# First-block attention of a two-block transformer kernel: heads zero-padded to 128 partitions, cumulated gates as extra contraction rows

## The chip, the cores and the metric

The kernel runs on one core of a Trainium2 chip. The metric is device time in microseconds of one launch. The kernel before has a median of 1077.13 us over three runs (1076.63 to 1077.66).

## The reference

The program computes two transformer blocks over 256 tokens of width 1024, in f32. Only the first block's mixer matters here. From the normalised input it makes, among others, queries, keys and values of eight "fox" heads of width 64 and queries of eight sliding-window ("swa") heads that share two key/value heads. The fox heads carry a forget gate: the logarithms of its sigmoid are summed over the sequence, and the difference of these sums is added to the scores.

```python
log_f = jax.nn.log_sigmoid(f_logit + f_bias)        # [256, 8 heads]
c = jnp.cumsum(log_f, axis=1)
logits = jnp.einsum('bqhd,bkhd->bhqk', qi, k) * HEAD_DIM ** -0.5
logits = logits + ci.transpose(0, 2, 1)[..., None] - c_k[:, :, None, :]
logits = jnp.where(causal, logits, NEG_INF)
p = jax.nn.softmax(logits, axis=-1)
out = jnp.einsum('bhqk,bkhd->bqhd', p, v)
```

The swa heads add a table bias and a sink to the softmax instead. Both outputs, with a short convolution, then go through gated output products.

## The kernel before

**Weights.** All matrices stream from memory in units of up to 1 MB (2048 columns of 128 partitions). SyncE loads a unit into one of three `raw` buffers as soon as VectorE has finished with the unit three before it (`fetch`). ScalarE rounds it to fp32r (`hi`, the line L1192), VectorE forms the rest (`lo`, L1785, a `tensor_tensor` of two SBUF inputs), and TensorE multiplies three times: high by high, high by low, low by high. In the program text both helpers convert unit u+2 where TensorE works on unit u. L547 is a feature-major unit (4 tiles of 128 columns, moving 256 tokens), L606 a token-major one (moving 512 columns).

**Order.** Every engine has its own hand-written sequence. TensorE goes: the fq units, fk, fv, svf (swa keys and values and the forget logits, 272 columns), sq, then cc, cu, cb (the convolution's inputs) and six gates of two units each.

**The gates' sums.** ScalarE copies svf's result out of PSUM (L1296, L1297). TensorE turns keys and logits over (L848, L849), VectorE adds the bias (L1887), ScalarE takes abs, exp and ln (L1301 to L1305), and a scan on VectorE gives `cumc`, [16 x 256] with the eight heads twice (L1893). Inside the second sq unit, TensorE turns `cumc` over (`cumulated_turned`, L838) into per-token columns `ct`.

**The head loop.** Sixteen heads, eight fox and then eight swa, are pipelined through slots: `attention(t)` stands on each engine behind the unit of slot t. On TensorE it holds `values(t-4)` (L819, L821), `probs(t-3)`, three transposes of the probabilities (L806), `scores(t-1)` (L787, L788) and, for fox heads, `decay(t)`. A fox head's queries and keys are 64 partitions of a tile that holds two heads, so the scores contract over 64 rows; the values have 64 columns and write 64 PSUM partitions. `decay` (L797) multiplies a [16 x 128] selection `oneh` (one row of -1, written by eight instructions at L1878) with `cumc`, which spreads the negated sums over 128 partitions. VectorE adds `ct` and the causal mask to it (`decays`, L1906, L1908) into `MC`, which `softmax` on VectorE (L1925, L1926) then adds to the scores while it takes the row maxima. ScalarE takes exponentials (L1315, L1316), VectorE scales (L1940, L1941), ScalarE copies the turned probabilities (L1323), and after every second head ScalarE and VectorE split the output of the pair (L1331, L1807). `values` of an even head waits for that split of the pair before; `scores` and `decay` wait for the maxima two heads before. Between its slots VectorE also does the whole convolution (L1977 to L1998), and ScalarE the gates' tanh (L1359).

**Evacuations.** `evac` on VectorE (L1825, L1827) multiplies four tiles of PSUM, [128 x 1024], by the row norms into fq, fk and sq. `evac_tm` on ScalarE (L1237) copies fv in two instructions of 512 columns. GpSimd has no program of its own.

## Time and profile before

| | us |
|---|---|
| median of three runs | 1077.13 |
| span of the profiled execution | 1075.8 |
| TensorE busy | 1065.3 (99%) |
| its weight port busy | 956.6 (89%) |
| VectorE busy | 752.9 (70%) |
| ScalarE busy | 602.0 (56%) |
| GpSimd busy | 0.2 |
| mean transfer rate | 170 GB/s |

PE is TensorE's multiply row, PEld its weight loads, DVE VectorE, ACT ScalarE, POOL GpSimd, SPq SyncE's queue of transfers. An f32 product appears as two records (two passes), so "L787 x2" is one product. In a shape such as 64*128 64x256 the first pair is contraction rows times stationary columns and the second the moving tile. "idle before <- releaser" in brackets tells what an engine last waited for. The mixer's head loop lies between 66 and 215 us of the span; the rest of the kernel is not touched by the diff.

### The profile page before, as it was taken

To read this page: it belongs to the slowest core of one execution; us is meant where nothing else is said; L and a number is where in the kernel's file an instruction comes from. 1 tells how busy PE (TensorE), PEld (TensorE's weight loads), DVE (VectorE), ACT (ScalarE), POOL (GpSimd) and SP (SyncE) were. 2 spreads that over 40 slices of the span, in tenths; PEclk is the share of its full clock that TensorE was granted. 3 is DMA by queue.
4 is the path that set the end of the run, shared out by engine and by line. 5 is a ranking of instruction groups with operands and counts; after the bars stand their busy time and mean duration, and the time that the engine had idled before them with its cause. 6 is when DMAs were issued, how large, how long until landed. Compare 5 with 4: busy or idle time off the path is not lost.

```text
span 1075.8 us, 16238 instructions
## 1 busy us (share of the span) xinstructions
PE 1065.3 (99%) x6866; PEld 956.6 (89%) x6866; DVE 752.9 (70%) x906; ACT 602.0 (56%) x731; POOL 0.2 (0%) x4
## 2 busy tenths in 40 slices
PE   8999999999999999999999999999999999999998
PEld 8988777789998988888889989999999888888887
DVE  5566855476745478777568898679947888776556
ACT  5454365543535465555446986589555665555444
POOL 0000000000000000000000000000000000000000
PEclk9999999999999999999999999999999999999999
DMA  9774244565553456664655545443544646654551
GB/s 303 187 223 153 79 157 157 161 191 194 171 183 118 156 178 224 195 191 153 212 189 176 154 143 167 143 151 125 157 158 148 196 141 212 196 193 160 198 174 40
DMA packets 141448, 183.08 MB, mean 170 GB/s; under 512 B 14132, under 2 KB 91936, under 8 KB 141376
## 3 DMA queue, kind: packets, MB, share of 16 engines
q1 hardware_dynamic: 141160, 181.85, 53.3%
q8 instruction: 54, 0.88, 0.3%
q10 hardware_dynamic: 216, 0.21, 0.1%
q14 instruction: 18, 0.15, 0.0%
HBM read 180.79 MB, written 1.25 MB: 169 GB/s over the span
## 4 chain that ended last, share of the span: by engine, by line
PE 93%; DVE 3%; ACT 2%; DMA 1%; issue 1%; DVEq 0%; ACTq 0%
PE ps L547 29%; PE ps L575 22%; PE ps L606 15%; PE ps L577 11%; PE ps L1012 3%; PE ps L652 2%; PE ps L1139 2%; PE ps L654 1%; PE ps L819 1%; DVE wlo L1785 1%; DMA raw<-in_w_in 1%; PE ps L806 1%; PE ps L788 1%; PE ps L901 1%; PE ps L1027 1%
## 5 line engine op out<-in xcount | busy, mean ns | idle before, releaser
L1785 DVE TENSOR_TENSOR wlo<-raw,whi 128x2048 fp32r<-128x2048 f32 (+3 forms) x170 | 378.3, 2228 | 163.6 <-ACT whi L1192 163.2
L1192 ACT ACTIVATE whi<-raw 128x2048 fp32r<-128x2048 f32 (+1 forms) x167 | 310.4, 1862 | 86.3 <-PE ps L577 34.2
L547 PE MATMUL ps<-ha,whi 128*128 128x256 f32 x1328 | 244.7, 286 | 2.3 <-DVE wlo L1785 2.2
L575 PE MATMUL ps<-ha,whi 128*128 128x512 f32 x640 | 222.7, 394 | 0.0
L547 PEld LDWEIGHTS ps<-ha,whi 128*128 128x128 f32 x1328 | 208.2, 193 | 6.5 <-issue 5.2
L547 PE MATMUL ps<-ha,wlo 128*128 128x256 f32 x664 | 188.5, 284 | 0.0
L577 PE MATMUL ps<-ha,wlo 128*128 128x256 f32 x640 | 177.4, 277 | 0.0
L575 PEld LDWEIGHTS ps<-ha,whi 128*128 128x128 f32 x640 | 120.0, 188 | 27.9
L547 PEld LDWEIGHTS ps<-ha,wlo 128*128 128x128 f32 x664 | 128.0, 193 | 0.0
L575 PE MATMUL ps<-pr,whi 128*128 128x512 f32 x352 | 122.1, 394 | 0.0
L577 PEld LDWEIGHTS ps<-ha,wlo 128*128 128x128 f32 x640 | 120.2, 188 | 0.1
L606 PE MATMUL ps<-whi,ha 128*128 128x512 f32 x320 | 100.6, 395 | 0.0
L577 PE MATMUL ps<-pr,wlo 128*128 128x256 f32 x352 | 97.5, 277 | 0.0
L575 PEld LDWEIGHTS ps<-pr,whi 128*128 128x128 f32 x352 | 66.0, 188 | 15.3
L606 PEld LDWEIGHTS ps<-whi,ha 128*128 128x128 f32 x320 | 58.7, 188 | 14.7 <-issue 3.3
L577 PEld LDWEIGHTS ps<-pr,wlo 128*128 128x128 f32 x352 | 66.1, 188 | 0.0
L606 PE MATMUL ps<-wlo,ha 128*128 128x512 f32 x160 | 62.5, 390 | 0.0
L1463 ACT ACTIVATE silu<-silu 128x512 f32<-128x512 f32 x22 | 13.9, 633 | 62.1 <-DVE silu L2124 62.1
L1458 ACT ACTIVATE silu<-ps 128x512 f32<-128x512 f32 x22 | 13.1, 598 | 41.8 <-PE ps L577 35.7
L606 PEld LDWEIGHTS ps<-wlo,ha 128*128 128x128 f32 x160 | 30.0, 188 | 6.6
L1012 PE MATMUL ps<-qt,kt 128*128 128x128 f32 x256 | 31.2, 275 | 0.4 <-DVE am L2242 0.4
L1012 PEld LDWEIGHTS ps<-qt,kt 128*128 128x128 f32 x256 | 30.3, 192 | 0.9 <-issue 0.6
(385 smaller groups left out, 1687.4 us busy)
## 6 DMA issues: line engine op xcount, KB each, us to landing
raw<-in_w_in SPq DMA_DIRECT2D x54, 1024.0 KB, 5.3
raw<-in_w_ffn_gate SPq DMA_DIRECT2D x11, 1024.0 KB, 5.1
raw<-in_w_ffn_up SPq DMA_DIRECT2D x11, 1024.0 KB, 5.2
raw<-in_w_gate SPq DMA_DIRECT2D x11, 1024.0 KB, 5.2
raw<-in_w_up SPq DMA_DIRECT2D x11, 1024.0 KB, 5.2
raw<-in_w_xkv SPq DMA_DIRECT2D x8, 1024.0 KB, 5.2
raw<-in_w_ffn_down SPq DMA_DIRECT2D x8, 1024.0 KB, 5.0
raw<-in_w_down SPq DMA_DIRECT2D x8, 1024.0 KB, 5.0
```

Of the source, the lines that this page charges most:

```text
L547: mm = e.matmul(ps[0:width, m * T:(m + 1) * T], a[:, kk, m * width:(m + 1) * width], b[:, off + k, :], start=k == 0 and j == 0 and m % 2 = ...
L575: e.matmul(banks[s][:, at_:at_ + 512], wh[:, kk, c], H[2][:, :, k, :], start=k == 0, stop=False, skip_group_check=True)
L577: mm = e.matmul(banks[s][:, at_ + T:at_ + 512], wl[:, kk, c], H[0][:, k, :], start=False, stop=k == K - 1, skip_group_check=True)
L606: mm = e.matmul(banks[s][:, t * 512:t * 512 + ncol], b[:, off + k, t * P:(t + 1) * P], a[:, kk, 0:ncol], start=k == 0 and j == 0, stop=k = ...
L652: e.matmul(banks[ss[i]][:, at_:at_ + 512], wh[:, k, c], H[2][:, :, k, :], start=k == 0, stop=False, skip_group_check=True)
L654: mm = e.matmul(banks[ss[i]][:, at_ + T:at_ + 512], wl[:, k, c], H[0][:, k, :], start=False, stop=k == 7, skip_group_check=True)
L1012: mm = e.matmul(Sb[w][:, m * P:(m + 1) * P], Kt[b][:, m, w * P:(w + 1) * P], Q_[:, m, wq_ * P:(wq_ + 1) * P], start=m == 0, stop=True, ski ...
L1139: mm = e.matmul(where, x[:, k, t_ * P:(t_ + 1) * P], w[:, kk, a:b], start=k == 0 and j == 0, stop=k == 7 and j == 2, skip_group_check=True)
L1192: e.activation(h, r, ACT.Copy).then_inc(*hi_done.up(n))
L1458: e.activation(silu[w][:, :, :], split_sums(ss[2 * (i % 2)])[1], ACT.Copy).then_inc(*a_evac.up(f"{b}g{i}"))
L1463: e.activation(silu[w][:, :, :], silu[w][:, :, :], ACT.Silu).then_inc(*a_stat.up((f"silu {b}", i)))
L1785: e.tensor_tensor(l, r, h.bitcast(F32), ALU.subtract).then_inc(*lo_done.up(n))
```

## The change

Each fox head gets a query tile, a key tile and a value tile of 128 partitions or columns: even heads use the lower half, odd heads the upper, and the other half is padding, so queries and keys become two tiles each (`fq[u]`, `fk[u]`, u the parity), as do fv, sq and sv. Four rows of the other half of each fox query and key tile carry the sums: in the key tile four rows hold the negated `cumc` of the four heads of that parity, against which the query tile has rows that are one for its own head and zero elsewhere; and the other way round for the query's own sums. The scores therefore come out of one product with the sums already in them. `decay`, `decays`, `cumulated_turned`, `oneh`, `ct` and `MC` go; `softmax` adds the plain causal mask `M3`.

A new program on GpSimd writes the pads: one-and-zero rows from the identity (four `tensor_copy` of [64 x 1024]) and zeros (six `memset` of a tile half, and one of `skf`). VectorE evacuates fq, fk and sq in two halves of 64 partitions (`evac_heads`) and writes the key sums; ScalarE writes fv in four instructions, svf in ten, and the query sums. The logits, their turning and the sums are now [128 x 256] tiles of which 16 rows count. The forget bias is loaded by four small transfers behind a wait for a memset of its column. The scores, 16 swa and fox alike, contract over 128 rows; all values have 128 columns, and the second head of a pair accumulates onto the first in the same PSUM tile. The first scores now wait for the key sums, the query sums and the pads.

```diff
+    OWN = [slice(0, 64), slice(64, 128)]
+    OTHER = [slice(64, 128), slice(0, 64)]
+    KEY_ROWS = [slice(64, 68), slice(0, 4)]
+    QUERY_ROWS = [slice(96, 100), slice(32, 36)]
...
+        e.wait_ge(*v_stat.on("constants"))
         for u in range(2):
-            e.dma_start(sc[8 * u:8 * u + 8, 16:17], d["forget_bias"].rearrange("a n -> n a")).then_inc(s_fb, 16)
+            bias_u = d["forget_bias"].rearrange("a (m u) -> m u a", u=2)[:, u, :]
+            e.dma_start(sc[KEY_ROWS[u], 16:17], bias_u, allow_slow_non_contiguous=True).then_inc(s_fb, 16)
+            e.dma_start(sc[QUERY_ROWS[u], 16:17], bias_u, allow_slow_non_contiguous=True).then_inc(s_fb, 16)
...
         def scores(i):
             kind, h = heads[i]
-            b, w = i % 2, kind == "fox"
-            S = Sb[b]
-            if w:
-                row = slice(64 * (h % 2), 64 * (h % 2) + 64)
-                qq, kk_ = fq[row, h // 2, :], fk[row, h // 2, :]
+            S = Sb[i % 2]
+            if kind == "fox":
+                qq, kk_ = fq[h % 2][:, h // 2, :], fk[h % 2][:, h // 2, :]
             else:
-                row = slice(64 * (h // 4), 64 * (h // 4) + 64)
-                qq, kk_ = sq_[row, h % 4, :], sk[row, :]
+                qq, kk_ = sq_[h // 4][:, h % 4, :], sk[:, :]
             if i == 0:
+                e.wait_ge(*p_pad.on("heads"))
                 e.wait_ge(*v_evac.on("fk"))
                 e.wait_ge(*a_evac.on(("fv", 1)))
                 e.wait_ge(*v_stat.on(("rows", "mem")))
+                e.wait_ge(*v_stat.on("key sums"))
+                e.wait_ge(*a_stat.on("query sums"))
             if i == 8:
+                e.wait_ge(*p_pad.on(("local value", 1)))
                 e.wait_ge(*v_evac.on("sq"))
                 e.wait_ge(*v_evac.on("sk"))
             if i >= 2:
                 e.wait_ge(*v_soft.on(("max", i - 2)))
-            if w:
-                e.wait_ge(*v_soft.on(("c", i)))
             e.matmul(S[:, 0:P], qq[:, 0:P], kk_[:, 0:P], start=True, stop=True, skip_group_check=True)
             e.matmul(S[:, P:P + T], qq[:, P:T], kk_[:, 0:T], start=False, stop=True,
                      skip_group_check=True).then_inc(*pe_score.up(("attn", i)))
-
-        def decay(i):
-            kind, h = heads[i]
-            if kind != "fox":
-                return
-            if i >= 2:
-                e.wait_ge(*v_soft.on(("max", i - 2)))
-            e.matmul(Sb[i % 2][:, 0:T], oneh[:, h, :], cumc[:, :], start=True, stop=True).then_inc(
-                *pe_score.up(("decay", i)))
...
         def values(i):
             kind, h = heads[i]
-            w = kind == "fox"
-            row = slice(64 * (h % 2), 64 * (h % 2) + 64) if w else slice(64 * (h // 4), 64 * (h // 4) + 64)
-            val, c = (fv, 64 * h) if w else (sv, 64 * (h // 4))
+            if kind == "fox":
+                val = [fv[h % 2][:, t_, h // 2, :] for t_ in range(2)]
+            else:
+                val = [sv[h // 4][:, t_, :] for t_ in range(2)]
             e.wait_ge(*a_soft.on(("pt", i)))
             if i == 8:
                 e.wait_ge(*a_evac.on("sv"))
             if i % 2 == 0 and i >= 2:
                 e.wait_ge(*v_split.on(("y", i - 1)))
-            e.matmul(Ob[row, 0:T], val[:, 0, c:c + 64], PT[i % 2][:, 0:T], start=True, stop=False,
-                     skip_group_check=True)
-            e.matmul(Ob[row, P:T], val[:, 1, c:c + 64], PT[i % 2][:, T:T + P], start=False, stop=True,
+            e.matmul(Ob[:, 0:T], val[0], PT[i % 2][:, 0:T], start=i % 2 == 0, stop=False, skip_group_check=True)
+            e.matmul(Ob[:, P:T], val[1], PT[i % 2][:, T:T + P], start=False, stop=True,
...
         def attention(t):
@@ -828,27 +816,15 @@
                 probs(t - 3)
             if 1 <= t < 17:
                 scores(t - 1)
-            if t < 16:
-                decay(t)
-
-        def cumulated_turned():
-            e.wait_ge(*v_stat.on("cumulated"))
-            e.wait_ge(*v_stat.on(("rows", "mem")))
-            for t_ in range(2):
-                mm = e.transpose(banks[3][:, 256 + 16 * t_:272 + 16 * t_], cumc[:, t_ * P:(t_ + 1) * P], ident[0:16, 0:16])
-            mm.then_inc(*pe_turn.up("cumulated"))
-            e.wait_ge(*v_stat.on("onehot"))
-            e.wait_ge(*a_evac.on(("fv", 1)))
-            attention(0)
 
         unit("sq", 0, HA, 0, None, v_evac.on("fq"))
         rows_of("mem", 3, v_split.on(("mem", 3)))
         e.wait_ge(*a_evac.on("sv"))
         for t_ in range(2):
-            e.transpose(banks[3][:, 512 + t_ * P:512 + (t_ + 1) * P], skf[:, t_, 0:P], ident[:, :])
-            mm = e.transpose(banks[3][0:16, 768 + t_ * P:768 + (t_ + 1) * P], skf[:, t_, P:P + 16], ident[:, :])
+            e.transpose(banks[3][:, 512 + t_ * P:512 + (t_ + 1) * P], skt[:, t_, :], ident[:, :])
+            mm = e.transpose(banks[3][:, 768 + t_ * P:768 + (t_ + 1) * P], skf[:, t_, :], ident[:, :])
         mm.then_inc(*pe_turn.up("sk"))
-        unit("sq", 1, HA, 0, middle=cumulated_turned)
+        unit("sq", 1, HA, 0)
...
-        evac_tm("fv", 2, lambda t_: fv[:, t_, :], 22)
+        e.wait_ge(*whole("fv"))
+        e.wait_ge(*p_pad.on("heads"))
+        for t_ in range(2):
+            v_t = banks[2][:, t_ * 512:t_ * 512 + 512].rearrange("p (m u c) -> p m u c", u=2, c=64)
+            for u in range(2):
+                mm = e.activation(fv[u][:, t_, :, OWN[u]], v_t[:, :, u, :], ACT.Copy, scale=sc[:, 22 + t_:23 + t_])
+            mm.then_inc(*a_evac.up(("fv", t_)))
...
-            e.activation(skf[:, t_, :], banks[1][:, 512 * t_ + P:512 * t_ + 272], ACT.Copy, scale=r_t)
-            mm = e.activation(sv[:, t_, :], banks[1][:, 512 * t_:512 * t_ + P], ACT.Copy, scale=r_t)
+            e.activation(skt[:, t_, :], banks[1][:, 512 * t_ + P:512 * t_ + T], ACT.Copy, scale=r_t)
+            for u in range(2):
+                by_parity = banks[1][:, 512 * t_ + T:512 * t_ + T + 16].rearrange("p (w m u) -> p u w m", w=2, u=2)[:, u]
+                e.activation(skf[:, t_, OTHER[u]].rearrange("p (w c) -> p w c", w=2)[:, :, 0:4], by_parity, ACT.Copy,
+                             scale=r_t)
+            for u in range(2):
+                mm = e.activation(sv[u][:, t_, OWN[u]], banks[1][:, 512 * t_ + 64 * u:512 * t_ + 64 * u + 64], ACT.Copy,
+                                  scale=r_t)
...
         hi(U["sq"][1][0] + 2)
+        e.wait_ge(*p_pad.on("heads"))
+        e.wait_ge(*v_stat.on("cumulated"))
+        for u in range(2):
+            r = QUERY_ROWS[u]
+            mm = e.activation(fq[u][r, :, :], cumc[r, :].unsqueeze(1).broadcast_to([4, 4, T]), ACT.Copy)
+        mm.then_inc(*a_stat.up("query sums"))
         attention(1)
...
+        def evac_heads(name, s, dst, scale):
+            e.wait_ge(*whole(name))
+            for u in range(2):
+                r = OWN[u]
+                mm = e.scalar_tensor_tensor(out=dst[u][r, :, :], in0=wide(banks[s][:, :])[r, :, :], scalar=scale,
+                                            in1=rows4(Rw)[r, :, :], op0=ALU.mult, op1=ALU.mult)
+            mm.then_inc(*v_evac.up(name))
...
-        evac("fq", 0, fq[:, :, :], Rw, 0.125)
+        evac_heads("fq", 0, fq, 0.125)
...
-        e.wait_ge(*v_stat.on("sel"))
-        for h in range(8):
-            mm = e.tensor_scalar(oneh[:, h, :], ones[0:16, :], sel[:, 8 + h:9 + h], -1.0, ALU.mult, ALU.mult)
-        mm.then_inc(*v_stat.up("onehot"))
...
-        e.wait_ge(s_fb, 32)
-        e.tensor_scalar(cA[0][:, :], banks[3][0:16, 768:1024], fb, None, ALU.add).then_inc(*v_stat.up("f logit"))
+        e.wait_ge(s_fb, 64)
+        e.tensor_scalar(cA[0][:, :], banks[3][:, 768:1024], fb, None, ALU.add).then_inc(*v_stat.up("f logit"))
         e.tensor_copy(sk[:, :], banks[3][:, 512:768]).then_inc(*v_evac.up("sk"))
...
-        def decays(i):
-            kind, h = heads[i]
-            if kind != "fox":
-                return
-            S, M = Sb[i % 2], MC[i % 2]
-            e.wait_ge(s_m3, 16)
-            e.wait_ge(*v_stat.on("ct"))
-            e.wait_ge(*pe_score.on(("decay", i)))
-            e.scalar_tensor_tensor(out=M[:, 0:P], in0=S[:, 0:P], scalar=ct[:, 0, h:h + 1], in1=M3[:, 0:P], op0=ALU.add,
-                                   op1=ALU.add)
-            e.scalar_tensor_tensor(out=M[:, P:3 * P], in0=S[:, 0:T], scalar=ct[:, 1, h:h + 1], in1=M3[:, P:3 * P],
-                                   op0=ALU.add, op1=ALU.add).then_inc(*v_soft.up(("c", i)))
...
             if w:
-                m0, m1 = MC[b][:, 0:P], MC[b][:, P:3 * P]
-                e.wait_ge(*v_soft.on(("c", i)))
+                m0, m1 = M3[:, 0:P], M3[:, P:3 * P]
+                e.wait_ge(s_m3, 16)
...
         rows_of("mem", Rm, 3)
-        e.wait_ge(*pe_turn.on("cumulated"))
-        e.tensor_copy(ct[:, :, :].rearrange("p t h -> p (t h)"), banks[3][:, 256:288]).then_inc(*v_stat.up("ct"))
-        attention(0)
+        e.wait_ge(*p_pad.on("heads"))
+        e.wait_ge(*v_stat.on("cumulated"))
+        for u in range(2):
+            r = KEY_ROWS[u]
+            mm = e.tensor_scalar(fk[u][r, :, :], cumc[r, :].unsqueeze(1).broadcast_to([4, 4, T]), -1.0, None, ALU.mult)
+        mm.then_inc(*v_stat.up("key sums"))
         lo(U["sq"][1][0] + 2)
-        evac("sq", 0, sq_[:, :, :], Rw, 0.125)
+        evac_heads("sq", 0, sq_, 0.125)
         attention(1)
...
+    def pool(e):
+        e.wait_ge(s_id, 16)
+        for u in range(2):
+            r = OTHER[u]
+            for what, dst, c in (("query", fq[u], KEY_ROWS[u].start), ("key", fk[u], QUERY_ROWS[u].start)):
+                e.tensor_copy(dst[r, :, :], ident[r, c:c + 4].unsqueeze(2).broadcast_to([64, 4, T])).then_inc(
+                    *p_pad.up((what, u)))
+                e.wait_ge(*p_pad.on((what, u)))
+            e.memset(fv[u][:, :, :, OTHER[u]], 0.0).then_inc(*p_pad.up(("value", u)))
+            e.wait_ge(*p_pad.on(("value", u)))
+        e.memset(skf[:, :, :], 0.0).then_inc(*p_pad.up("heads"))
+        for u in range(2):
+            e.wait_ge(*p_pad.on("heads" if u == 0 else ("local value", 0)))
+            e.memset(sq_[u][OTHER[u], :, :], 0.0).then_inc(*p_pad.up(("local query", u)))
+            e.wait_ge(*p_pad.on(("local query", u)))
+            e.memset(sv[u][:, :, OTHER[u]], 0.0).then_inc(*p_pad.up(("local value", u)))
+
```

## Rows read from the trace of the kernel before

**Rows 1.** Section 1 of the page: busy time, share of the span, instructions.

```profile
PE 1065.3 (99%) x6866; PEld 956.6 (89%) x6866; DVE 752.9 (70%) x906; ACT 602.0 (56%) x731; POOL 0.2 (0%) x4
```

**Rows 2.** Chain of waits (start us, us, what), one block of a fox head.

```profile
101.64 0.58 PE ps L819 x2
...
102.43 0.48 PE ps L806 x3
102.91 0.41 PE ps L787 x2
103.32 0.43 PE ps L788 x2
103.76 0.62 PE ps L797 x2
104.38 5.95 PE ps L547 x48
```

**Rows 3.** Chain of waits: transposes with no values ahead; two token-major units.

```profile
85.19 0.33 PE ps L806 x3
...
192.04 5.69 PE ps L606 x24
...
199.00 5.47 PE ps L606 x24
```

**Rows 4.** Timeline of the weight port, 55 to 63 us: a whole unit between these.

```profile
56.18 0.30 PEld L547 LDWEIGHTS ps<-ha,whi 128*128 128x128 f32 x2 [0.31 <-issue]
...
61.93 0.54 PEld L625 LDWEIGHTS ps<-n_tm,ones 128*128 128x128 f32 x4
```

**Rows 5.** Timeline of all engines, 58 to 71 us: the cumulated gates, first score.

```profile
58.17 0.36 ACT L1296 ACTIVATE skf<-ps,sc 128x144 f32<-128x144 f32 x1
...
61.16 2.29 DVE L1785 TENSOR_TENSOR wlo<-raw,whi 128x2048 fp32r<-128x2048 f32 x1 [0.17 <-ACT whi L1192]
...
63.36 0.47 DVE L1887 TENSOR_SCALAR ca<-ps,sc 16x256 f32<-16x256 f32 x1
...
65.18 1.89 ACT L1192 ACTIVATE whi<-raw 128x2048 fp32r<-128x2048 f32 x1
...
65.37 0.68 DVE L1893 TENSOR_TENSOR_SCAN cumc<-cb,ca 16x256 f32<-16x256 f32 x1 [1.01 <-ACT ca L1305]
...
66.51 0.26 PE L838 MATMUL ps<-ident,cumc 16*128 16x16 f32 x2 [0.55 <-DVE rm L1820]
...
70.29 0.49 PE L787 MATMUL ps<-fk,fq 64*128 64x128 f32 x2
```

**Rows 6.** Timeline, VectorE: the sq evacuation and the scaling of the probabilities.

```profile
97.54 0.35 DVE L1941 TENSOR_SCALAR lb<-lb,sc 128x256 f32<-128x256 f32 x1
...
70.40 1.23 DVE L1827 SCALAR_TENSOR_TENSOR sq<-ps,rw 128x1024 f32<-128x1024 f32 x1
```

**Rows 7.** Timeline of VectorE, 100 to 170 us: maxima, decay, outputs' low halves.

```profile
103.94 0.29 DVE L1925 CUSTOM_DVE_ANT_0 lb<-ps,mc 128x128 f32<-128x128 f32 x1 [0.63 <-PE ps L788]
...
106.50 0.35 DVE L1906 SCALAR_TENSOR_TENSOR mc<-ps,ct,m 128x128 f32<-128x128 f32 x1
...
155.21 0.42 DVE L1807 TENSOR_TENSOR y_lo<-ps,y_hi 128x256 fp32r<-128x256 f32 x1
...
169.18 0.42 DVE L1807 TENSOR_TENSOR y_lo<-ps,y_hi 128x256 fp32r<-128x256 f32 x1
```

**Rows 8.** Chain of waits: the values of the ninth head.

```profile
158.69 0.58 PE ps L819 x2
```

**Rows 9.** Timeline, first 26 us: SyncE's bias loads; TensorE's fk unit.

```profile
9.71 0.67 SPq L446 DMA_DIRECT2D sc<-in_forget_bias  x2
...
24.14 0.56 PE L547 MATMUL ps<-ha,whi 128*128 128x256 f32 x2 [1.96 <-DVE wlo L1785]
```

**Rows 10.** Chain of waits: the transfer of fk's first unit.

```profile
11.70 8.04 DMA raw<-in_w_in
```

**Rows 11.** Windows (busy us of each engine, granted clock, DMA share, GB/s), 24 to 28 us.

```profile
24.00:28.00 4.00, 3.86 (x20) 3.89 (x21) 3.76 (x4) 0.15 (x1) 0.00 (x0) 0.57 1.03 381
```

More of the change, by code:

```diff
@@ L49, in constants @@
     bucket = np.where(dist < 16, np.maximum(dist, 0), np.minimum(large, 31))
-    small = np.zeros((32, 896), np.float32)
+    small = np.zeros((32, 768), np.float32)
     small[:, 0:384] = (np.arange(32)[:, None] == bucket[None, :]) & inside[None, :]
     small[0:8, 384:768] = np.where(inside, 0.0, NEG)[None, :]
-    for r in range(16):
-        second = float(r >= 8)
-        small[r, 768] = second
-        small[r, 769] = -(1.0 - second)
-        small[r, 776 + r % 8] = 1.0 - second
-        small[r, 784 + r % 8] = second
     return {"c_big": big, "c_masks": masks, "c_small": small}
@@ L132, in build @@
     mk = at("mk", [P, 7, P], F32, 160)
-    g_tm = at("g_tm", [P, P], F32, 170)
+    g_tm = at("g_tm", [P, P], F32, 181)
     gates = at("gates", [P, 6, 2, 512], F32, 160)
-    fq = at("fq", [P, 4, T], F32, 184)
-    fk = at("fk", [P, 4, T], F32, 188)
-    fv = at("fv", [P, 2, 512], F32, 192)
-    sq_ = at("sq", [P, 4, T], F32, 196)
-    sk = at("sk", [P, T], F32, 200)
-    sv = at("sv", [P, 2, 128], F32, 201)
-    cA = [at(f"ca{i}", [16, T], F32, 202 + i) for i in range(2)]
-    cB = at("cb", [16, T], F32, 204)
-    oneh = at("oneh", [16, 8, P], F32, 176)
-    MC = [at(f"mc{i}", [P, 384], F32, 180 + 1.5 * i) for i in range(2)]
-    ct = at("ct", [P, 2, 16], F32, 95.5)
-    cumc = at("cumc", [16, T], F32, 206)
-    skf = at("skf", [P, 2, 144], F32, 96)
+    fq = [at(f"fq{u}", [P, 4, T], F32, 164 + 4 * u) for u in range(2)]
+    fk = [at(f"fk{u}", [P, 4, T], F32, 172 + 4 * u) for u in range(2)]
+    skf = at("skf", [P, 2, P], F32, 180)
+    fv = [at(f"fv{u}", [P, 2, 4, P], F32, 184 + 4 * u) for u in range(2)]
+    sq_ = [at(f"sq{u}", [P, 4, T], F32, 192 + 4 * u) for u in range(2)]
+    sk = at("sk", [P, T], F32, 200)
+    sv = [at(f"sv{u}", [P, 2, P], F32, 201 + u) for u in range(2)]
+    cA = [at(f"ca{i}", [P, T], F32, 203 + i) for i in range(2)]
+    cB = at("cb", [P, T], F32, 205)
+    cumc = at("cumc", [P, T], F32, 206)
+    skt = at("skt", [P, 2, P], F32, 96)
     z = at("z", [P, 4, T], F32, 96)
@@ L154, in build @@
     PT = [at(f"pt{i}", [P, 384], F32, 140.5 + 1.5 * i) for i in range(2)]
-    small = at("small", [32, 896], F32, 120)
+    small = at("small", [32, 768], F32, 120)
     bt = at("bt", [8, 384], F32, 124)
@@ L527, in arrived, with unit @@
             e.wait_ge(*lo_done.on(n))
-        def unit(name, i, H, s, ready=None, free=None, K=8, nm=4, width=P, off=0, middle=None):
+        def unit(name, i, H, s, ready=None, free=None, K=8, nm=4, width=P, off=0):
             n, k0, nk = U[name][i]
@@ L553, in unit @@
                     mm.then_inc(*half_done.up((name, 0)))
-                    if middle is not None:
-                        middle()
         def piece(name, H, s, ready=None, free=None, K=8, last=False, middle=None):
@@ L1302, in scalar @@
         e.wait_ge(*a_stat.on("f abs"))
-        e.activation(cA[1][:, :], cA[1][:, :], ACT.Exp, bias=zero[0:16, :], scale=-1.0).then_inc(*a_stat.up("f exp"))
+        e.activation(cA[1][:, :], cA[1][:, :], ACT.Exp, bias=zero, scale=-1.0).then_inc(*a_stat.up("f exp"))
         e.wait_ge(*a_stat.on("f exp"))
@@ L1850, in vector @@
         e.tensor_tensor(bt[:, :], banks[3][0:8, 0:384], small[0:8, 384:768], ALU.add).then_inc(*v_stat.up("bt"))
-        e.tensor_copy(sel, small[0:16, 768:792]).then_inc(*v_stat.up("sel"))
         diagonal("x", 22)
@@ L2521, in _ @@
             vector(e)
+        @block.gpsimd
+        def _(e):
+            pool(e)
 _INS = ["x", "mem", "mix_norm_g", "w_in", "forget_bias", "conv_w", "sink", "w_branch", "w_mix_out", "rel_bias",
```

11 lines of the change are left out of this document (5 added, 6 removed).

## The prediction

> **What bounds the kernel now.** I read the page's busy times first: TensorE is busy for 99% of the span [rows 1], so a change pays here only by what it takes out of TensorE's own row of work, and it costs what TensorE is newly made to wait for. Second, the chain of waits between 60 and 215 us: with the head loop running it is TensorE at nearly every step, one slot of the loop being a weight unit and then one head's block [rows 2]. Third, the timeline of ScalarE and VectorE around 56 to 72 us, where the cumulated gates are made, and around 104 to 156 us, where VectorE does the convolution; there one sees how far the helpers are from being late. Last, the first 25 us, which hang on transfers.
>
> **TensorE, part by part.** A price without any change of operand shape comes first. Three transposes behind a weight unit take 0.33 us [rows 3]: 0.11 us for a pass of 128 columns. An f32 product has two passes, so 128 columns should cost 0.22 and 256 columns 0.43; the second score product, whose shape is that of the product before it, does cost 0.43 [rows 2]. A unit of 48 x 2 fp32r products that follows nothing smaller takes 61.93 - 56.18 = 5.75 us [rows 4]; half of it, behind a decay product, takes 5.95 where 48 x 0.12 = 5.75 was due, and a token-major unit takes 5.69 behind a score and 5.47 behind a transpose [rows 2, 3]. So wherever the shape of the stationary or of the contraction changes, 0.15 to 0.22 us is lost:
> first value product (128x64) 0.58 against 0.43: 0.15, 16 times, 2.4 us;
> transposes behind values 0.48 against 0.33: 0.15, 15 times, 2.25;
> first score (64 rows) 0.41 against 0.22: 0.20, 16 times, 3.2;
> decay product (16 rows) 0.62 each, 8 times, with 0.19 of switch in it, 5.0 with the work itself;
> return to 128x128 for the next unit: 0.20 to 0.22, 17 times behind scores or the first decay, once behind the last values, 3.7.
> The change makes scores and values 128x128 and drops the decay product, so all of it goes: 16.5 us. The padded products stream the same columns as before, so I price them at 0.22 and 0.43. I take the unswitched rows for them, though no row here has an f32 product of 256 columns with 128 rows; a bound from the other side is the 0.58 of today's values, which over 32 products would give back 4.8 us.
>
> **The stage that makes the cumulated gates (56 to 72 us).** Taken out: the two small transposes with their wait inside the second sq unit, 0.55 to 0.72 idle and 0.15 of work, 0.9 us [rows 5]. The eight one-hot rows and the copy of the turned sums go from VectorE; they were hidden and give nothing. Put in: ScalarE's evacuations. One of 144 columns takes 0.36 us, about 0.25 from start to start [rows 5]; fv becomes four instead of two (+0.4) and svf ten instead of four, most of them short (+0.9 us, bounds 0.6 to 1.5). ScalarE has no slack from the fv evacuation to the conversion of cc's first unit, so the first sq unit starts 0.4 later (it waits for its conversion), and VectorE's pass over that unit (2.29, from 61.16) moves by 1.3 to 1.4 to about 62.5. Behind it VectorE has the gate logit, which starts today at 63.36 and would start at about 64.85; the scan, today at 65.37 for 0.68, ends at about 67.5 [rows 5].
> Then come the new rows. ScalarE first converts cc's second unit (1.89) and then writes the query sums, 2 x [4 x 1024]. By the conversion's 2048 columns in 1.89 a 1024-column pass is 0.95: 66.7 + 1.9 + 1.95 = 70.6. TensorE ends the second sq unit at about 63.25 + 5.75 = 69.0 and now waits there about 1.7 us, with the first score at 70.7 instead of 70.29 [rows 5]. So this stage's removed 0.9 is more than used up: the first score is 0.4 later. VectorE writes the key sums, 2 x 1024 from SBUF; between 0.7 each (if the 0.35 for 256 columns of the scaling in rows 6 grows slowly) and 1.2 each (the rate of the evacuation in rows 6); I take 0.75, as the scaling is the same instruction. Both halves of each head evacuation cost a full 1024 columns, so fq, fk and sq each pay another 1.23 [rows 6]. For fq and fk TensorE is one to two units away and the one-hot writes that go balance one of them: nothing. For sq it delays VectorE when it is already late.
>
> **Who is late next.** With TensorE faster, VectorE's line of work decides. I followed both from the new first score. TensorE alone would end the fifth block's scores at 103.76 - 4.9 + 0.4 = 99.3 (four blocks at 1.02, 1.02, 1.02 and 1.32 and a part of 0.5) [rows 2]. VectorE, with key sums, the pass over cc's second unit, the doubled sq evacuation, then softmax, ScalarE's exponentials and conversion, and the next pass each in turn, starts that head's maxima at about 100.2, today 103.94 [rows 7]: 3.7 earlier. From there to the low half of the seventh head's output, today done at 155.21 + 0.42 = 155.63, no step in the trace waits for TensorE, and only two of the removed decay pairs (0.65 from start to next, first one at 106.50) lie on it [rows 7]: 5.0 earlier in all, at 150.6. TensorE would be 10.8 earlier by then (4.5 up to here, two slots at 1.32, one remainder of 0.82, four token-major slots at 0.72) and reach the values that need that output at 147.9 instead of 158.69 [rows 8]. It waits 2.7 us, there or at one of the two waits before it. Afterwards ScalarE and VectorE need 13.97 us for two units (from 155.21 to 169.18 [rows 7], where they wait only for each other) against TensorE's 2 x (5.47 + 1.63) = 14.2, so the lag does not grow.
>
> **The start.** Four tiny loads of the forget bias stand where two stood, at 0.34 each from issue to issue [rows 9]; SyncE issues the fourth weight load behind them 0.7 later. The chain from the second low pass over an 8.04 us transfer to the unit that begins at 24.14 is bound by transfers [rows 9, 10], so most of the 0.7 arrives there; while it restarts, TensorE is granted 0.57 of full clock over four microseconds, which is mostly its lower level of 1.2 GHz instead of 2.4 [rows 11]; I leave that cost as it is today. I take 0.45, between 0 and 0.7. GpSimd, idle so far, fills pads during the same 20 us, and VectorE's low passes feed that chain. No row shows GpSimd beside VectorE. Bounds: 0, and 2.3 if each of the two passes before the transfer takes twice as long; I take 0.6.
> The Trainium skill, "GPSIMD Engine Reference", Key points, says that GpSimd shares its SBUF interfaces with VectorE and contends with instructions that have two SBUF inputs, which these low passes are. No run here shows it so far; by that rule the sum would be nearer its upper bound, without it 0.6 us shorter than mine.
>
> **Sum.** 16.5 + 0.9 - 0.4 - 1.7 = 15.3; less 2.7 for the late output, less 0.45 and 0.6 at the start: 11.5 us. The profiled span of 1075.8 becomes 1064.3. The median of the runs is 1.3 above that span: 1065.6 us.
>
> **Rivals.**
> A, the forecast, 1065.6, own range 1062.9 to 1068.5. Chance 0.62.
> B, the helpers are not late (shorter ScalarE evacuations, cheap pads): none of the 2.7 and 1.05 is paid: 1077.1 - 15.3 = 1061.8. For it: my clock of VectorE is a sum of ten estimates. Against: slack at the seventh output is 3.1 us today and TensorE gains 10.8. Chance 0.12.
> C, GpSimd and VectorE get in each other's way in the first 25 us and the low passes stretch to double, or TensorE's 1.7 us of idle at 69 us is followed by a lower clock, as 1.96 us of idle before 24.14 was (4 us at 0.57 cost 1.7) [rows 9, 11]: 2 to 4 us more, 1067.6 to 1069.6. Against the second: helpers are late afterwards anyway and hide part of it. Chance 0.15.
> D, the change does not do what it says: the gaps belong to the waits in front of these products, not to their shape. Then only the decay products with their two gaps go, 8 x 0.82 = 6.5, less 1.2 in the gate stage and 1.05 at the start: 1072.9. Against it: transposes behind a wait but behind no other shape cost 0.33, and a unit behind them 5.47 [rows 3]. Chance 0.07.
> E, slower: GpSimd's pads are late. ScalarE's fv evacuation, at about 49.2 us, waits for seven GpSimd instructions that can begin when the identity has landed, near 4.7. Up to 6.4 us each they are hidden; every microsecond more on each is 7 us on the path; from 8 us each the kernel is slower than before. At 10 us each: 1065.6 + 25 = 1091. Against: VectorE does 1024 columns in 1.23 [rows 6], and this would be eight times that. Chance 0.04.
>
> **How the numbers follow.** Range 1061.5 to 1070.5: all of A and B and nearly all of C; D and E, 0.11, are left out, as is a margin for wrongly sized terms. About 0.2% (2 us) is what a measurement of this kernel tells from no change. A, B, C and D are all faster by more: 0.94 with a little of D and C taken off for a second late helper, 0.02 within, 0.04 slower.
>
> **What would show it.** In the profile after: first value product about 0.43, transposes 0.33 in every block, first score 0.22, next unit without an idle weight port; a whole block about 1.63 us. TensorE idle 1 to 2 us ahead of the first score at about 70. Waits of TensorE on VectorE's output split or low pass between 125 and 155 us, 2 to 3 us together. GpSimd busy some 10 us before 25 us. The prediction is wrong if the score's 0.41 stays with 128 rows, if VectorE's wait ahead of the unit at 24 us grows by over 1.5 us, or if the waits in the head loop sum to over 5 us.

## The result, and the profile after

The kernel after takes 1065.63 us, median of 4 runs (1062.82 to 1068.1), beside 1076.88 us for the kernel before, median of 4 (1074.8 to 1077.66). The ratio is 0.9887, 95% interval 0.9866 to 0.9909: 9.8 to 14.4 us faster, where 11.5 was forecast. The profiled execution has a span of 1063.7 us against 1075.8.

Page of the kernel after, section 1 (busy us, share of the span, instructions). Against [rows 1], GpSimd has 11 instructions and 7.8 us more, and TensorE 14.3 us less:

```profile
PE 1051.0 (99%) x6848; PEld 959.7 (90%) x6848; DVE 750.7 (71%) x886; ACT 604.4 (57%) x741; POOL 8.0 (1%) x15
```

Chain of waits of the kernel after (start us, us, what), one slot of the loop, to be laid beside [rows 2]:

```profile
88.40 0.43 PE ps L808 x2
88.84 0.22 PE ps L809 x2
89.06 0.33 PE ps L794 x3
89.39 0.22 PE ps L784 x2
89.61 0.43 PE ps L785 x2
90.04 5.75 PE ps L547 x48
```

The reader is to see that every product now has the price that its columns set and nothing on top: first values 0.43 for 0.58, transposes 0.33 for 0.48, first score 0.22 for 0.41, no decay product, the unit 5.75 for 5.95. The whole block is 1.63 us.

Timeline of the kernel after (start us, us, engine line operation, idle before and its releaser), the stage of the cumulated gates, beside [rows 5]:

```profile
58.40 1.97 ACT L1168 ACTIVATE whi<-raw 128x2048 fp32r<-128x2048 f32 x1
...
62.61 0.48 DVE L1885 TENSOR_SCALAR ca<-ps,sc 128x256 f32<-128x256 f32 x1
...
64.43 1.90 ACT L1168 ACTIVATE whi<-raw 128x2048 fp32r<-128x2048 f32 x1
...
64.63 0.69 DVE L1891 TENSOR_TENSOR_SCAN cumc<-cb,ca 128x256 f32<-128x256 f32 x1 [1.01 <-ACT ca L1293]
...
65.84 1.38 DVE L1945 TENSOR_SCALAR fk<-cumc 4x1024 f32<-4x1024 f32 x2 [0.21 <-DVE rm L1814]
...
66.36 2.12 ACT L1334 ACTIVATE fq<-cumc 4x1024 f32<-4x1024 f32 x2
...
68.62 0.46 PE L784 MATMUL ps<-fk,fq 128*128 128x128 f32 x2 [1.67 <-ACT fq L1334]
```

TensorE stands still for 1.67 us until ScalarE has written the query sums. ScalarE had them to write from 65.3 on, when the scan ended, but was converting a weight until 66.3.

TensorE's waits between 60 and 215 us in the kernel after (line waited for: us in total, times, longest):

```profile
PE ps L784 <- ACT fq L1334: 1.7, 1, 1.7
PE ps L808 <- DVE y_lo L1801: 1.3, 2, 0.8
```

The second line is the late output half that was forecast. The kernel before had neither; it had 0.6 us for the turned sums.

**The account of the two profiled executions**, by TensorE's own records. Up to the start of the unit of [rows 9] (24.14, now 23.46) 0.7 us are gained. From there to the end of the fk units it is 13.25 us before and 11.75 after: 1.5 gained, since the kernel before had half the clock for 3.4 us there and the kernel after did not. From that end to the first score 0.5 is lost (32.90 us, now 33.41). From the first score to the last attention product 12.7 us are gained. In the first feed-forward stage 2.6 us are lost. The rest of the span differs by 0.2, all of it at the unit behind the last values, which has no change of shape in front of it any more. The sum is 12.1. Three of these, the first, second and fifth, also differ between executions of one and the same kernel, as the next run shows.

### The profile page after: what moved, and what is told of

The parts are those of the page before. It is cut to its first block, busy times and chain, and to the rows that moved or that the text cites. A ratio compares the mean times of both kernels' runs of the same rounds, so it can differ in the third digit from the quotient of the medians.

```text
span 1063.7 us, 16194 instructions
## 1 busy us (share of the span) xinstructions
PE 1051.0 (99%) x6848; PEld 959.7 (90%) x6848; DVE 750.7 (71%) x886; ACT 604.4 (57%) x741; POOL 8.0 (1%) x15
## 4 chain that ended last, share of the span: by engine, by line
PE 88%; DVE 4%; ACT 4%; issue 2%; DMA 1%; DVEq 0%; SPq 0%; ACTq 0%
PE ps L547 28%; PE ps L573 22%; PE ps L604 13%; PE ps L575 11%; PE ps L988 3%; PE ps L650 2%; PE ps L1115 2%; ACT whi L1168 2%; DVE wlo L1779 1%; PE ps L652 1%; DMA raw<-in_w_in 1%; PE ps L877 1%; PE ps L1003 1%; PE ps L899 1%; PE ps L614 1%
## 5 line engine op out<-in xcount | busy, mean ns | idle before, releaser
L573 PE MATMUL ps<-ha,whi 128*128 128x512 f32 x640 | 224.1, 395 | 0.0
L575 PE MATMUL ps<-ha,wlo 128*128 128x256 f32 x640 | 179.4, 280 | 0.0
L573 PEld LDWEIGHTS ps<-ha,whi 128*128 128x128 f32 x640 | 120.0, 188 | 27.7
L573 PE MATMUL ps<-pr,whi 128*128 128x512 f32 x352 | 123.3, 395 | 0.0
L575 PEld LDWEIGHTS ps<-ha,wlo 128*128 128x128 f32 x640 | 121.1, 189 | 0.1
L575 PE MATMUL ps<-pr,wlo 128*128 128x256 f32 x352 | 98.9, 281 | 0.0
L573 PEld LDWEIGHTS ps<-pr,whi 128*128 128x128 f32 x352 | 66.0, 188 | 15.4
L604 PEld LDWEIGHTS ps<-whi,ha 128*128 128x128 f32 x320 | 59.4, 188 | 12.5 <-issue 0.8
L575 PEld LDWEIGHTS ps<-pr,wlo 128*128 128x128 f32 x352 | 66.7, 189 | 0.0
```

Source lines behind the costliest of these rows:

```text
L573: e.matmul(banks[s][:, at_:at_ + 512], wh[:, kk, c], H[2][:, :, k, :], start=k == 0, stop=False, skip_group_check=True)
L575: mm = e.matmul(banks[s][:, at_ + T:at_ + 512], wl[:, kk, c], H[0][:, k, :], start=False, stop=k == K - 1, skip_group_check=True)
L604: mm = e.matmul(banks[s][:, t * 512:t * 512 + ncol], b[:, off + k, t * P:(t + 1) * P], a[:, kk, 0:ncol], start=k == 0 and j == 0, stop=k = ...
```

## The experiments

**Once more.** The kernel after, measured again, to see which parts of the account repeat.

> The changed kernel once more, unaltered, for its spread and a second profile. If the agreement of the first result with the forecast is due to the terms named, the median is again 1063 to 1068 us. In the first profile two things were not in the forecast: the start was 2.2 us quicker by the end of the fk units (no lower clock at 24 us, transfer 7.18 us), and the first feed-forward stage ran about 2.3 us longer than in the kernel before. If both belong to the change they come again (fk units done near 35.2 us, feed-forward pairs slower by 1.5%); if they are a matter of the execution they come and go between runs of the same kernel.

It took 1064.21 us (1062.81 to 1067.63, 5 runs), ratio 0.9894 (0.9878 to 0.991) to 1076.28 for the kernel before (11 runs). Its span was 1065.8, 2.1 above that of the other profile of the same kernel, and the account says why: this time it did have the half clock for 3.4 us near 25 us, and its first feed-forward stage was as fast as before's, while the second was 3.0 slower. Windows (us, busy us of each engine with its instructions, granted clock, DMA share, GB/s) of the first stage, the kernel after:

```profile
440.00:480.00 40.00, 40.00 (x228) 34.67 (x228) 29.67 (x29) 20.64 (x22) 0.00 (x0) 1.00 0.59 192
480.00:520.00 40.00, 40.00 (x228) 34.73 (x227) 24.00 (x22) 19.77 (x19) 0.00 (x0) 1.00 0.56 182
```

The same windows of the same kernel measured again, and one of its second stage:

```profile
440.00:480.00 40.00, 40.00 (x233) 34.99 (x232) 29.78 (x29) 21.06 (x23) 0.00 (x0) 1.00 0.58 187
480.00:520.00 40.00, 40.00 (x233) 34.94 (x232) 24.80 (x23) 20.38 (x19) 0.00 (x0) 1.00 0.59 188
...
940.00:980.00 40.00, 40.00 (x228) 34.68 (x227) 28.91 (x27) 19.13 (x19) 0.00 (x0) 1.00 0.52 171
```

TensorE is busy throughout, its granted clock is full in all of them, and it issues 228 products in 40 us in one execution and 233 in another. I take a stage from the first to the last of its 992 products of L573 and L575 (L575 and L577 in the kernel before). Over all twelve profiles of this study the first stage takes 173.3 or 175.9 us and the second 173.0 or 176.2 to 176.3, with nothing between. Four profiles had the first stage slow, four the second, four neither and none both. So 2.6 to 3 us between two spans of this kernel mean nothing by themselves, and each experiment below is also read on the stretch that it changes. One thing stays open: of the ten profiles of kernels with padded heads eight have a slow stage, and of the two of kernels with narrow heads none has. Two profiles are too few to say that the pace has nothing to do with the change, or that it has.

**Values over 64 columns.** The kernel after, with the value products narrow again.

```diff
-                val = [fv[h % 2][:, t_, h // 2, :] for t_ in range(2)]
+                val = [fv[u][:, t_, h // 2, row] for t_ in range(2)]
...
-            e.matmul(Ob[:, 0:T], val[0], PT[i % 2][:, 0:T], start=i % 2 == 0, ...
-            e.matmul(Ob[:, P:T], val[1], PT[i % 2][:, T:T + P], start=False, ...
+            e.matmul(Ob[row, 0:T], val[0], PT[i % 2][:, 0:T], start=True, ...
+            e.matmul(Ob[row, P:T], val[1], PT[i % 2][:, T:T + P], start=False, ...
```

> The changed kernel with the value products back at 64 columns and 64 PSUM partitions; all else as changed. Theory (price of a shape change): first value product 0.58 instead of 0.43, transposes behind it 0.48 instead of 0.33, the unit behind the last values 0.22 more, 4.9 us of TensorE in all, of which the 2.4 before the ninth head's values only fill time in which TensorE waits for VectorE: 2.5 us slower than the changed kernel (range 2.2 to 4.9). Rival (the gaps belong to the waits in front): unchanged, 0 us.

1066.65 us (1063.99 to 1068.1), ratio 0.9911 (0.9897 to 0.9925). Chain of waits of this kernel, one slot:

```profile
163.09 0.58 PE ps L810 x2
163.66 0.22 PE ps L811 x2
163.88 0.48 PE ps L794 x3
164.36 0.22 PE ps L784 x2
164.58 0.43 PE ps L785 x2
```

The 0.58 and the 0.48 are back, the scores keep their 0.22 and 0.43. To read such a loss apart from the two scattering stages I take the time from the first score to one fixed product, the 5000th from the end, which lies ahead of them (at 289.73 us in the kernel after). Here it is 2.7 us longer than in the kernel after (223.80 against 221.11). The loss by the forecast's terms is 2.4 + 2.25 = 4.65. Laid beside the kernel after product by product, 2.0 of it disappears because TensorE now waits less for VectorE: 0.77 at the values of the seventh head (132.8 us in the kernel after), 0.66 at those of the ninth (148.2), and 0.35 and 0.18 at two weight units that waited for their low pass (126.5 and 141.7). That leaves the 2.7 measured. Rival D, by which these gaps belong to waits, gives 0 here.

**The local heads' scores over 64 rows.**

```diff
-                qq, kk_ = sq_[h // 4][:, h % 4, :], sk[:, :]
+                row = OWN[h // 4]
+                qq, kk_ = sq_[h // 4][row, h % 4, :], sk[row, :]
```

> The changed kernel with only the eight swa scores contracting over 64 rows again. Theory: first score 0.41 instead of 0.22 and 0.22 more on the unit behind, 8 x 0.42 = 3.4 us of TensorE, of which 1.3 in waiting time: 2.1 us slower than the changed kernel (2.0 to 3.4). Rival (gaps belong to the waits): 0 us; its second form (only f32 products of 16 rows pay): 0 us as well.

1064.64 us (1063.34 to 1067.34), ratio 0.9898 (0.9882 to 0.9913). Chain of waits of this kernel, and of the kernel after behind it:

```profile
163.43 0.43 PE ps L809 x2
163.86 0.22 PE ps L810 x2
164.08 0.33 PE ps L795 x3
164.41 0.42 PE ps L785 x2
164.82 0.43 PE ps L786 x2
165.26 5.66 PE ps L604 x24
```

```profile
163.65 0.22 PE ps L784 x2
163.87 0.43 PE ps L785 x2
164.31 5.48 PE ps L604 x24
```

There are two switches of about 0.19, one into the 64 rows (0.42 for 0.22) and one out (5.66 for 5.48). Over eight heads that is 3.0 us of TensorE, a little under the expected 3.4. The stretch from the first score to the fixed product is 1.9 us longer, since the rest fills waits; the expected range began at 2.0. The whole-kernel medians, 0.4 apart, cannot tell it.

**The decay products alone.** The kernel before, without its eight decay products and what VectorE does for them. It leaves the cumulated gates out of the scores, so its result is another one; it is here for its time alone.

```diff
-            if w:
-                e.wait_ge(*v_soft.on(("c", i)))
...
-            if t < 16:
-                decay(t)
...
-                m0, m1 = MC[b][:, 0:P], MC[b][:, P:3 * P]
+                m0, m1 = M3[:, 0:P], M3[:, P:3 * P]
```

> The kernel before without its decay products and VectorE's decay pairs; scores take only the causal mask, so the differences of the cumulated gates are left out of the result. Everything else stays narrow. Theory: 7 slots at 0.82 and the first at 0.72 plus the work it hid, 6.5 us faster than before, 1070.4 us (1069 to 1071), VectorE not late at the ninth head. Rival (the decay product is the whole change and the padding is worth nothing): it reaches the changed kernel's 1065.6.

1069.87 us (1068.76 to 1072.21), ratio 0.9949 (0.9935 to 0.9963), which is 5.5 us on this run's 1076.28; the medians themselves are 6.4 apart. By the records it is 0.5 in the gate stage and 4.4 behind the first score, 4.9 together. Chain of waits of this kernel:

```profile
94.75 0.58 PE ps L817 x2
95.33 0.22 PE ps L819 x2
95.54 0.48 PE ps L804 x3
96.02 0.41 PE ps L785 x2
96.44 0.43 PE ps L786 x2
96.87 5.94 PE ps L547 x48
```

Compared with [rows 2] only the 0.62 has gone. The 0.41 and the unit's 0.2 over 5.75 stay, so they belong to the scores' 64 rows and not to the decay product. A slot gives 0.62 and not the 0.82 of rival D. The expectation above had 0.82 too, and with it 6.5 us: its median came out in the stated range, its price of a slot did not hold, since the unit now follows a score of 64 rows and pays the 0.2 all the same. All in all the decay products are two fifths of what the change brings by the records (4.9 of 12.2 from the end of the fk units to the last attention product), and about half by the medians.

**Pads later.** GpSimd begins its pads at 8.3 us instead of 2.65, so that its copies meet VectorE's low passes.

```diff
         e.wait_ge(s_id, 16)
+        e.wait_ge(*hi_done.on(0))
```

> The changed kernel with GpSimd's pads begun only when ScalarE has converted the first weight unit, at about 8.2 us instead of 2.6, so that its copies of [64 x 1024] run beside VectorE's low passes, which have two SBUF inputs. In the changed kernel as it is, only one memset falls beside such a pass (1.22 us against 1.21 before). If GpSimd and VectorE contend, the passes of 1024 columns at 8.5 and 10.5 us take over 1.3 us and up to 2.4; if they do not, 1.21 to 1.23 us, and GpSimd's copies stay at 1.03.

Timeline of this kernel, GpSimd and VectorE:

```profile
8.33 1.04 POOL L2493 COPY fq<-ident 64x1024 f32<-64x1024 f32 x1 [7.89 <-ACT whi L1246]
8.50 1.95 DVE L1779 TENSOR_TENSOR wlo<-raw,whi 128x1024 fp32r<-128x1024 f32 x1
...
9.43 1.92 POOL L2493 COPY fk<-ident 64x1024 f32<-64x1024 f32 x1
```

Timeline of the kernel after, the same instructions:

```profile
6.52 1.03 POOL L2492 COPY fk<-ident 64x1024 f32<-64x1024 f32 x1
...
8.50 1.22 DVE L1779 TENSOR_TENSOR wlo<-raw,whi 128x1024 fp32r<-128x1024 f32 x1
8.57 0.96 POOL L2500 MEMSET sq<- 64x1024 f32 x1
...
10.46 1.23 DVE L1779 TENSOR_TENSOR wlo<-raw,whi 128x1024 fp32r<-128x1024 f32 x1
```

Beside a GpSimd copy the low pass takes 1.95 us instead of 1.22, and the copy 1.92 instead of 1.03; beside a memset (8.57, in the kernel after) the pass keeps its 1.22. This bears out the rule of the Trainium skill ("GPSIMD Engine Reference", Key points) that was weighed in the prediction, for the copies. The records look like turns: the first copy keeps its 1.04, the pass that began during it ends 1.08 us behind that copy's end (10.45, 9.37), and the second copy, begun during the pass, ends 0.90 behind the pass (11.35). In the kernel after the copies are over by 7.55 us, before the first such pass, so it costs nothing. The kernel as a whole took 1064.77 us in its one run, no later than the kernel after: the unit of [rows 9] began at 22.71, without any wait, although its low passes had been slowed.

**Work in the waits for exponentials.** In the kernel after VectorE waits in every softmax for ScalarE's exponentials. Here the two halves of the sq evacuation, cc's evacuation and scaling, the masks' cast and half of the convolution's taps are put into those waits.

```diff
+            if i in fill:
+                fill[i]()
             e.wait_ge(*a_soft.on(("exp", i)))
...
-        evac_heads("sq", 0, sq_, 0.125)
...
+        fill.update({0: sq_half(0), 1: sq_half(1), 2: cc_evac, 3: cc_scaled, 4: cast_masks,
+                     5: lambda: taps(2), 6: lambda: taps(3)})
```

> The changed kernel with VectorE's order altered and nothing else: the two sq halves, cc's evacuation and scaling, the mask cast and two of the four convolution tiles go into the 1.05 us in which VectorE waits for ScalarE's exponentials of heads 0 to 6. Theory (TensorE waits in the head loop because VectorE's line of work is late): the waits of 0.5 to 1.2 us at the blocks near 126, 132 and 147 us of the changed kernel vanish, first score to last unit of the loop 2 to 2.5 us shorter, 2 us faster than the changed kernel, 1062 to 1062.5 as a median. Rival (ScalarE's conversions or the transfers set those waits): the waits stay, 0 to 0.3 us.

1063.13 us (1060.28 to 1064.55), ratio 0.9863 (0.984 to 0.9886). TensorE's waits between 60 and 215 us in this kernel:

```profile
PE ps L784 <- ACT fq L1334: 2.1, 1, 2.1
```

The line on the output half is gone, and from the first score to the fixed product it takes 218.83 us against 221.11: 2.3 less. That is the cost of the late VectorE in the kernel after, forecast at 2.7. Product by product, 1.04 of it stood at the ninth head's values, 0.77 at the seventh's, and 0.35 and 0.18 at the two weight units near 126.5 and 141.7 us. The median of 1063.13 misses the expected 1062 to 1062.5 by a little; this profile has a slow second feed-forward stage.

**The wait ahead of the first score, first try.** The query sums move from ScalarE to GpSimd, once in the kernel with filled waits (two labels, the second a repeat) and once in the plain kernel after.

```diff
+        e.wait_ge(*v_stat.on("cumulated"))
+        for u in range(2):
+            r = QUERY_ROWS[u]
+            e.tensor_copy(fq[u][r, :, :], cumc[r, :].unsqueeze(1).broadcast_to([4, 4, T])).then_inc(
```

> The kernel named fill with the query sums written by GpSimd instead of ScalarE, right behind the scan. Theory (TensorE's 1.7 us of idle ahead of the first score is ScalarE's order: a conversion of 1.9 and then two passes of 1.06): GpSimd, at 1.03 us a pass and beginning when the scan ends, has them ready about 1 us sooner; the idle falls to 0.7 us and, as nothing is late behind it any more, the kernel is 1 us faster than fill. Rival (the first score waits for VectorE's key sums or GpSimd is slow to start): idle stays at 1.2 or more, 0 to 0.5 us.

> The changed kernel with only the query sums on GpSimd. Theory (in the changed kernel the late line of VectorE decides, not the first score): the first score comes 1 us sooner but the waits near 132 and 147 us grow by as much, 0 to 0.4 us faster. Rival (TensorE's time simply adds up): 1 us faster.

With filled waits 1060.86 us (1059.32 to 1062.96) and, repeated, 1062.82 (1060.36 to 1064.08); without, 1064.48 (1063.19 to 1069.18). The expected microsecond did not come. The first of these medians is 2.3 us under that of the kernel with filled waits alone, but from the end of the fk units to the first score only 0.3 is gained (33.53 us for 33.80), the stretch behind it is the same (218.84), and the repeat, at 1062.82, agrees with the 1063.13 as was expected of it. In the plain kernel the stretch behind the first score grew from 221.11 to 221.68, with one new wait of 0.3 us, for ScalarE's copy of turned probabilities. Timeline of the first of them:

```profile
64.25 2.48 POOL L2526 COPY fq<-cumc 4x1024 f32<-4x1024 f32 x2 [53.20 <-DVE cumc L1885]
...
64.64 2.64 DVE L1943 TENSOR_SCALAR fk<-cumc 4x1024 f32<-4x1024 f32 x2 [0.20 <-DVE rm L1808]
...
67.53 0.46 PE L784 MATMUL ps<-fk,fq 128*128 128x128 f32 x2 [1.79 <-DVE fk L1943]
```

GpSimd does start 0.1 us behind the scan, but the two engines now write at the same time, and VectorE's key sums take 2.64 us instead of 1.38. TensorE waits 1.79 for VectorE where it waited 2.05 for ScalarE with filled waits alone; without them it is 1.80 for 1.67. This theory of the gain fell; a new wait took the place of the old.

**Second try.** Filled waits, and the query sums stay on ScalarE but go ahead of its conversion.

```diff
-        hi(U["sq"][1][0] + 2)
         e.wait_ge(*p_pad.on("heads"))
...
         mm.then_inc(*a_stat.up("query sums"))
+        hi(U["sq"][1][0] + 2)
```

> The kernel named fill with ScalarE's two query-sum passes ahead of its conversion of cc's second unit. Theory (the idle ahead of the first score is ScalarE's order; on GpSimd the same writes did not help because they and VectorE's key sums slowed each other, 2.48 and 2.63 us instead of 2.06 and 1.38): the sums start when the scan ends, are ready 1 us sooner and leave VectorE at 1.38; idle 1.0 instead of 2.0 us, and as the conversion is needed only 6 us later nothing else waits: 1 us faster than fill. Rival (the moved conversion makes VectorE's line late again): the waits near 126 to 147 us come back and it is no faster than fill.

1059.51 us (1058.31 to 1061.95, 5 runs) beside 1076.56 (9 runs), ratio 0.9848 (0.9832 to 0.9863). Timeline of this kernel:

```profile
63.97 2.12 ACT L1333 ACTIVATE fq<-cumc 4x1024 f32<-4x1024 f32 x2 [0.89 <-DVE cumc L1891]
...
64.41 1.38 DVE L1949 TENSOR_SCALAR fk<-cumc 4x1024 f32<-4x1024 f32 x2 [0.21 <-DVE rm L1814]
...
66.24 0.46 PE L784 MATMUL ps<-fk,fq 128*128 128x128 f32 x2 [0.75 <-ACT fq L1333]
...
68.07 2.29 DVE L1779 TENSOR_TENSOR wlo<-raw,whi 128x2048 fp32r<-128x2048 f32 x1 [2.28 <-ACT whi L1168]
```

The wait ahead of the first score is 0.75 us, and the loop behind it takes 218.83 us as with filled waits alone, though the next low pass starts at 68.07 only. It is the fastest version of all, 0.5% under the kernel after (1059.5 against 1064.2 to 1065.6, measured at other times), and 3.3 us under the repeat of the first try, measured beside it. The order of the query sums accounts for 1.3 us against filled waits alone (32.50 for 33.80 us from the end of the fk units to the first score), where 1 was expected; this profile also had neither the half clock nor a slow feed-forward stage.

## Why the prediction held, point by point

The median was forecast at 1065.6 and measured at 1065.63. The closeness is luck in part: the start came out better than its terms by 1.5 us or more, and a slow feed-forward stage hid that. The mechanism behind the other terms is not luck.

**TensorE's 16.5 us.** Every price of the sum is in the chain of the kernel after to 0.01 or 0.02 us, and the two kernels that undo one part each bring the forecast gaps back (0.58 and 0.48 to 0.01 us; the way out of a 64-row score costs 0.18 for 0.22). The open point of the forecast, whether a two-pass product of 256 columns with 128 rows costs 0.43, is settled: it does. The bound of 4.8 us given back did not apply. The prediction speaks of a unit of 48 x 2 products and of half of it; both of its rows are one unit of 48 products, so the price of 5.75 stands.

**The gate stage.** Forecast: the first score 0.4 later against TensorE's units, with a wait of 1.7 in front of it; measured 0.5 and 1.67. The units ahead ended 2.18 us sooner here (35.21 against 37.39, see the account); with that taken off, the gate logit was due at 62.67, the end of the scan at 65.3, the second conversion at 64.5 and the end of the query sums at 68.4, and they stand at 62.61, 65.32, 64.43 and 68.48. A [4 x 1024] pass costs ScalarE 1.06 and not 0.95, VectorE 0.69 and not 0.75.

**Who is late next.** VectorE, at the output halves, in the place named. The forecast was 2.7 us, the experiment that takes the cause away says 2.3. The ninth head's values were forecast 10.8 - 2.7 = 8.1 us earlier against the units of the start, and came 8.3 earlier; they waited for the output half there (0.80), and the other such wait (0.54) is two slots before. The low pass was late as well, at the two weight units named above. Rival B, by which the helpers are not late, falls.

**The start: the step that failed.** I charged 0.45 for two more small loads and 0.6 for GpSimd beside VectorE. The loads do push the fourth weight's issue from 10.42 to 11.43 us, but the transfer of [rows 10] is the fifth, which waits for the second low pass and not for the loads. Chain of waits of the kernel after, around its issue:

```profile
10.50 1.20 DVE wlo L1779
11.70 0.13 SPq L417
...
11.87 7.18 DMA raw<-in_w_in
```

The fifth was issued 0.2 us behind the end of that pass, where the kernel before needed 0.03. Over the ten profiles with four bias loads this delay is 0.03 to 0.84 us, in six of them under 0.25; where it is 0.84, in the repeat, the queue had stood behind the loads. The two added loads take 0.67 from issue to issue, so they cost the chain between nothing and 0.67, mostly less than the 0.45 charged. The transfer then took 7.18 us where it had taken 8.04 [rows 10] and landed 0.7 sooner; and the low passes kept their 1.22. Over all the profiles that transfer takes 5.6 to 8.0 us and the unit of [rows 9] begins anywhere from 21.76 to 24.14 us, both ends of it without the change's loads, which is more than the term itself. What sets the transfer's time is open. The GpSimd term is 0, for a reason that lies in the order: in the profile after the identity has landed by 2.65 us, the four copies are over by 7.55, and the low pass of 1024 columns that feeds the chain starts at 8.50. I had put the start of the pads near 4.7; with that start the copies would have reached into the pass, at the price that the late pads showed, 0.73 us.

**What hid the miss.** The repeat of the kernel after had the half clock at 25 us as the kernel before had, so the two compare with only its slow second stage taken off, which costs 3.0 us (866.54 us behind the last attention product, against 863.55 in the profile of the second try, where no stage is slow). The spans are then 1075.8 and 1065.8 - 3.0 = 1062.8: 13.0 us. Of these, 12.5 lie behind the fk units, where the forecast's terms come to 15.3 - 2.7 = 12.6, and 0.5 lies ahead of them, where the forecast had a loss of 1.05. So in this pair the start alone is off, by 1.5 us, of which at most 1.05 can be the two terms; the rest is this stretch's own scatter of 2.4 us. The medians of five and four runs differ by 12.1 and 11.3, nearer to the forecast 11.5. That would fit the slow stages in most profiles of the kernels with padded heads, but no trace of the other runs shows it. In the profiled pair the start came 2.2 us early and the first feed-forward stage 2.6 late, which cancel.

**The rivals.** D fell to three kernels. C's second half, a lower clock behind the wait ahead of the first score, did not come: no profile has one there. C's first half is a real effect, which the change escapes because its copies end 1 us before the pass. E did not come: the copies take 1.03 us each where 6.4 were allowed.

## What to carry to other kernels

Where products of several shapes alternate on TensorE, price each against the same product behind one of its own shape: in this kernel a change of rows or columns cost 0.15 to 0.2 us, nearly as much as 128 columns of an f32 product (0.22), and zeros in a 128x128 operand were cheaper. Then follow the slowest helper to where its slack ends, since a part of the gain goes there, and give its work the places where it waits anyway. Before moving work to an idle engine, look at what runs beside it: GpSimd beside VectorE made both slower by about the amount that the move was to save.

## What the runs showed of the hardware that I had not expected

A GpSimd copy of [64 x 1024] and a VectorE pass with two SBUF inputs slow each other from 1.03 to 1.92 us and from 1.22 to 1.95, the later one waiting for the earlier as it seems; VectorE's key sums, which have one input, suffer too (1.38 to 2.64 for two of [4 x 1024] beside copies); a memset beside a pass with two inputs does not disturb it (1.22). The rule of the Trainium skill ("GPSIMD Engine Reference", Key points) names VectorE instructions with two SBUF inputs and those in a 2-port perf mode. The runs show it for the first kind. The key sums have one input and contend all the same; whether they ran in such a mode no run here shows.

The half clock of [rows 11] came and went between executions of one kernel: of twelve profiles two had it, one of the kernel before and one of the kernel after, for 3.4 us from about 24.5 us, at a cost of about 1.5 us. TensorE's wait ahead of it was 1.96 us in the one and 1.94 in the other; in the ten profiles without it that wait was 0 to 1.79 us. After 1.66 to 2.05 us of idle ahead of the first score no profile shows it.

Each feed-forward stage of the same instructions, at full granted clock and with TensorE always busy, runs at one of two paces in an execution, 233 or 228 products in 40 us where it was looked at, 2.6 us apart over the first stage and 3.2 over the second. DMA share and rate don't tell the two apart (0.59 and 188 GB/s in one fast window, 0.59 and 192 in a slow one). What sets it is open, and so is whether the change has a part in it; it makes a single profile's span of this kernel good to about 3 us only.
